# Loading the first attention head earlier in a one-core Trainium2 encoder kernel: second buffer, moved weight splits, reordered loads

## What is computed

```
kv = x @ w_kv;  k = rope(kv[:, :1024]);  v = kv[:, 1024:]      # 8 heads, two key maps of 64 per head
q  = rope(x @ w_q) * 64**-0.5
lam = exp(sum(lam0*lam1)) - exp(sum(lam2*lam3)) + lambda_init
p0, p1 = softmax(q0 @ k0.T), softmax(q1 @ k1.T)                # block-causal mask, per head
o  = rms_norm((p0 - lam*p1) @ v, g_norm) * (1 - lambda_init)
x  = layer_norm(ALPHA * x + o @ w_o)
```

## Time and profile before

| | us |
|---|---|
| runs | 2978.02 (median), 2977.02, 4519.82 |
| profiled execution, its time | 2981.81 |
| profiled execution, its span | 2980.0 |
| mean granted TensorE clock | 0.984 of full |
| TensorE busy | 2873.8 (96%) |

### The profile page before, as it was taken

How to read it: one execution, slowest core, us unless ns; L and a number is a source line. 1 busy time by engine, 2 the same in 40 slices (tenths; PEclk the granted TensorE clock), 3 DMA queues, 4 the chain that set the end, 5 groups by cost and what they waited for, 6 DMA issues and landing times. The chain is left out here.

```text
span 2980.0 us, 40342 instructions
## 1 busy us (share of the span) xinstructions
PE 2873.8 (96%) x15644; PEld 2543.4 (85%) x15644; DVE 1214.8 (41%) x2185; ACT 864.4 (29%) x1738; POOL 841.2 (28%) x939
## 2 busy tenths in 40 slices
PE   8999898999999999999999899988999999999997
PEld 8878777899988998897888688866899899989996
DVE  2256744632222222236513477743462222222226
ACT  2153241322211221122101278743241122112222
POOL 2112260521211121124212177831341111111114
PEclk9999998999999999999999999998999999999999
DMA  4111405111111111110232534294121111111101
GB/s 130 58 29 52 139 31 202 43 57 43 42 42 42 42 43 44 40 43 29 82 109 92 179 110 116 86 351 182 43 71 43 43 42 42 42 42 42 42 29 64
DMA packets 207186, 223.92 MB, mean 75 GB/s; under 512 B 42816, under 2 KB 151616, under 8 KB 207056
## 3 DMA queue, kind: packets, MB, share of 16 engines
q1 hardware_dynamic: 207056, 222.16, 23.0%
HBM read 184.90 MB, written 37.22 MB: 75 GB/s over the span
## 5 line engine op out<-in xcount | busy, mean ns | idle before, releaser
L792 POOL TENSOR_TENSOR wsplit<-raw,wsplit 128x1024 fp32r<-128x1024 f32 x192 | 459.4, 2395 | 1717.8 <-ACT wsplit L1030 1652.1
L1432 PE MATMUL ps<-xt,wsplit 128*128 128x384 f32 x5184 | 904.6, 334 | 1.4 <-DVE xt L1899 1.4
L1432 PEld LDWEIGHTS ps<-xt,wsplit 128*128 128x128 f32 x5184 | 899.1, 188 | 3.1 <-DVE xt L1899 1.8
L1623 PE MATMUL ps<-wsplit,hT 128*128 128x512 f32 x3456 | 787.7, 389 | 0.0
L1623 PEld LDWEIGHTS ps<-wsplit,hT 128*128 128x128 f32 x3456 | 649.0, 188 | 134.3
L1450 PE MATMUL ps<-wsplit,xt 128*128 128x512 f32 x2592 | 602.7, 393 | 2.8 <-DVE xt L1899 2.8
L1450 PEld LDWEIGHTS ps<-wsplit,xt 128*128 128x128 f32 x2592 | 487.9, 189 | 110.9 <-issue 6.5
L1030 ACT ACTIVATE wsplit<-raw 128x1024 fp32r<-128x1024 f32 x184 | 193.9, 1054 | 882.7 <-PE ps L1623 615.7
L2103 DVE TENSOR_TENSOR x_res<-x_res,ps 128x512 f32<-128x512 f32 x252 | 173.0, 687 | 434.8 <-PE ps L1623 434.8
L2155 DVE TENSOR_SCALAR hsq<-ps 128x384 f32<-128x384 f32 x192 | 107.0, 557 | 537.0 <-PE ps L1432 537.0
L1172 ACT ACTIVATE hsq<-hsq 128x384 f32<-128x384 f32 x192 | 101.1, 527 | 547.8 <-DVE hsq L2155 547.8
(11 more groups left out here) (186 smaller groups left out, 2365.1 us busy)
## 6 DMA issues: line engine op xcount, KB each, us to landing
raw<-in_w_up SPq DMA_DIRECT2D x64, 512.0 KB, 4.0
raw<-in_w_down SPq DMA_DIRECT2D x64, 512.0 KB, 3.7
Kc<-in_cache_k SPq DMA_DIRECT2D x8, 2048.0 KB, 10.1
Vc<-in_cache_v SPq DMA_DIRECT2D x8, 2048.0 KB, 10.1
raw<-in_w_in_a SPq DMA_DIRECT2D x24, 512.0 KB, 3.7
out<-kvs SPq DMA_DIRECT2D x36, 256.0 KB, 2.0
raw<-in_w_kv SPq DMA_DIRECT2D x16, 512.0 KB, 4.9
q_scr<-qst SPq DMA_DIRECT2D x16, 512.0 KB, 2.6
```

The source lines that it names most:

```text
L792: nc.gpsimd.tensor_tensor(wsplit[:, slot, 1, :], raw[:, slot, :], wsplit[:, slot, 0, :].bitcast(F32), ALU.subtract).then_inc(lo_done, 1)
L1432: last = nc.tensor.matmul(ps[0:M, b, 0:GW], st, xt[:, c, k, ng * GW:(ng + 1) * GW], start=(k == 0 and i == 0), stop=(k == KT - 1 and i == 2))
L1623: last = nc.tensor.matmul(ps[:, (v + t) % 6, :], hT[:, a, 2 * kp + k, tok:tok + P], wsplit[:, q, b, k * 512:(k + 1) * 512], start=(kp == 0 ...
```

## The change

The buffer `kqd2` is added, behind the query buffer in the region of the values; pairs 2 and 3 (the second half of head 0's tokens) use it, all others `kqd`. Pairs 0 and 2 (keys of head 0) and the two small loads for lambda and the norm gain are issued at the end of unit 3's turn in SP's program, pairs 1 and 3 (queries of head 0) after the stores of unit 4. Pair 4 now waits for the turns of pair 0 only, pair 5 for those of pair 1. SP no longer waits for the store of the last stream queries before the attention; those waits move to steps 16 and 40, with the load of `kqS`. The load of the first half of `w_o_b` moves behind the first values; its splits move to steps 6, 14, 22, 30 (ScalarE) and 8, 16, 24, 32 (GpSimd). Lambda's sums move to the start of unit 4 on DVE, its exponential ahead of unit 5's queries on ScalarE. At the end, attended tiles 0 to 5 are loaded ahead of `sample_out(6)`, tiles 6 and 7 after the last stream product, and then the last two outputs are stored.

```diff
@@ buffers
+    kqd2 = at("kqd2", O_V + 26624, [P, 2, 4, 2, 2, HD])
@@ SP: pair_in
-            if i >= 2:
-                sp.wait_ge(turned_full, 2 * i - 2)
+            kq = kqd2 if i in (2, 3) else kqd
+            if i >= 4:
+                sp.wait_ge(turned_full, 2 * i - 2 if i >= 6 else 2 * i - 6)
@@ SP: units of the products
-        load_p(G_O2, w_o_b[0], 0)
-        sp.wait_ge(ln_done, 2 * TILES)
-        for i in range(6):
-            sp.wait_ge(kv_out[i], 16 * 2 * TILES // 6)
-        pair_in(0)
+            if u == 3:
+                sp.wait_ge(ln_done, 2 * TILES)
+                for i in range(6):
+                    sp.wait_ge(kv_out[i], 16 * 2 * TILES // 6)
+                pair_in(0)
+                pair_in(2)
+                sp.dma_start(lamt[:], ...).then_inc(lam_in, 16)
+                sp.dma_start(gcol, ...).then_inc(lam_in, 16)
         for i in range(3):
             sp.wait_ge(q_out[i], 16 * ((PT - i + 2) // 3))
         pair_in(1)
-        sp.dma_start(lamt[:], ...).then_inc(lam_in, 16)
-        sp.dma_start(gcol, ...).then_inc(lam_in, 16)
+        pair_in(3)
         for t in range(TILES):
             kv_store(5, t)
         for i in range(6):
-            sp.wait_ge(kv_out[i], 16 * (6 if i % 3 < 2 else 7))
+            sp.wait_ge(kv_out[i], 16 * 6)
...
-        pair_in(2)
-        for i in range(3):
-            sp.wait_ge(q_out[i], 16 * Q_STORES[i])
-        pair_in(3)
         sp.wait_ge(g_full, GU_O2)
         values_in(0)
         pair_in(4)
+        pair_in(5)
         values_in(1)
-        pair_in(5)
         values_in(2)
+        load_p(G_O2, w_o_b[0], 0)
@@ SP: end of the stream attention
-        for b in range(STREAMS - 3, STREAMS - 1):
-            sample_out(b)
+        sample_out(STREAMS - 3)
         for i in range(2):
             sp.wait_ge(o_out[i], 16 * H_B * PT // 2)
         sp.wait_ge(smp_s_full, 2 * STREAMS)
-        for t in range(PT):
-            if t == 6:
-                sp.wait_ge(smp_pv, 2 * STREAMS)
-            sp.dma_start(oin[:, t, :], o_scr[t]).then_inc(tile_in[t], 16)
-        sample_out(STREAMS - 1)
+        for t in range(6):
+            attended_in(t)
+        sp.wait_ge(smp_pv, 2 * STREAMS)
+        for t in range(6, PT):
+            attended_in(t)
+        for b in range(STREAMS - 2, STREAMS):
+            sample_out(b)
@@ GpSimd, in step s
-            if 2 <= s < 6:
-                split_lo(G_O2 + s - 2)
+            if s % PT == 0 and 1 <= s // PT <= 4:
+                split_lo(G_O2 + s // PT - 1)
@@ ScalarE, in step s
-            if 0 <= s < 4:
-                split_hi_scaled(G_O2 + s)
+            if s % PT == 6 and s < 4 * PT:
+                split_hi_scaled(G_O2 + s // PT)
```

More of the change, by code:

```diff
@@ L647, in pair_in @@
                     for c in range(2):
-                        sp.dma_start(kqd[:, 0, :, c, dup, :], src[:, :, c]).then_inc(pair_loaded[0], 16)
+                        sp.dma_start(kq[:, 0, :, c, dup, :], src[:, :, c]).then_inc(pair_loaded[0], 16)
             else:
                 src = q_scr[4 * part:4 * part + 4, :, 2 * h:2 * h + 2].rearrange("t p c s d -> p t (c s d)")
-                sp.dma_start(kqd[:, 1].rearrange("p t c s d -> p t (c s d)"), src).then_inc(pair_loaded[1], 16)
+                sp.dma_start(kq[:, 1].rearrange("p t c s d -> p t (c s d)"), src).then_inc(pair_loaded[1], 16)
         def kv_store(u, t):
@@ L669, in _ @@
                     kv_store(u - 1, t)
-        load_p(G_O2, w_o_b[0], 0)
-        sp.wait_ge(ln_done, 2 * TILES)
-        for i in range(6):
-            sp.wait_ge(kv_out[i], 16 * 2 * TILES // 6)
-        pair_in(0)
+            if u == 3:
[4 more added lines that the diff above has]
+                pair_in(2)
+                sp.dma_start(lamt[:], lam[0:1].broadcast_to([P, 4, HD])).then_inc(lam_in, 16)
+                sp.dma_start(gcol, g_norm_b.rearrange("o v -> v o")).then_inc(lam_in, 16)
         for i in range(3):
@@ L678, in _ @@
         pair_in(1)
-        sp.dma_start(lamt[:], lam[0:1].broadcast_to([P, 4, HD])).then_inc(lam_in, 16)
-        sp.dma_start(gcol, g_norm_b.rearrange("o v -> v o")).then_inc(lam_in, 16)
+        pair_in(3)
         for t in range(TILES):
@@ L721, in _ @@
                 values_in(s // PT + 3)
-            if s == PT:
+            if s == 2 * PT:
+                for i in range(3):
+                    sp.wait_ge(q_out[i], 16 * Q_STORES[i])
+            if s == 5 * PT:
+                for i in (2, 5):
+                    sp.wait_ge(kv_out[i], 16 * 7)
                 sp.wait_ge(lo_done, G_O2 + 4)
@@ L752, in _, with attended_in @@
                 sample_out(b - 3)
-        for b in range(STREAMS - 3, STREAMS - 1):
-            sample_out(b)
+        def attended_in(t):
+            sp.dma_start(oin[:, t, :], o_scr[t]).then_inc(tile_in[t], 16)
+        sample_out(STREAMS - 3)
         for i in range(2):
@@ L1260, in _ @@
         split_hi(G_KVQ + 23)
+        act.wait_ge(lam_p, 2)
+        nc.scalar.activation(lam2, lam2, ACT.Exp).then_inc(lam_e, 1)
         for t in range(PT):
             query_hi(5, t)
-        act.wait_ge(lam_p, 2)
-        nc.scalar.activation(lam2, lam2, ACT.Exp).then_inc(lam_e, 1)
         def split_hi_scaled(g):
@@ L1735, in prepare @@
                 pe.wait_ge(*turned(i - 1 if i > 8 else i - 4))
+            kq = kqd2 if 4 <= i < 8 else kqd
             for k in range(4):
                 last = nc.tensor.transpose(ps[:, p_bank(i), k * P:(k + 1) * P],
-                                           kqd[:, int(mat == "q"), k, c].rearrange("p a d -> p (a d)"), ident)
+                                           kq[:, int(mat == "q"), k, c].rearrange("p a d -> p (a d)"), ident)
             last.then_inc(turned_full, 1)
@@ L2286, in query_lo, with lambda_sums @@
                                            ALU.mult, ALU.subtract).then_inc(q_split, 1)
+        def lambda_sums():
+            dve.wait_ge(lam_in, 32)
+            for i in range(2):
+                nc.vector.tensor_tensor(lamp[:, i, :], lamt[:, 2 * i, :], lamt[:, 2 * i + 1, :], ALU.mult).then_inc(dve_steps, 1)
+            dve.wait_ge(dve_steps, 2)
+            for i in range(2):
+                nc.vector.reduce_sum(lam2[:, i:i + 1], lamp[:, i, :], AX.X).then_inc(lam_p, 1)
+            nc.vector.tensor_scalar(gcol, gcol, 1.0 - LAMBDA_INIT, None, ALU.mult).then_inc(dve_steps, 1)
         nr = [0]
         for u in range(6):
+            if u == 4:
+                lambda_sums()
             for t in range(TILES):
@@ L2327, in _ @@
                     query_lo(2 * PT - 1)
[L2330 to L2336, removed]
         dve.wait_ge(lam_e, 1)
```

## The result

The kernel after takes 2966.88 us (median of six runs, 2965.61 to 2969.32), the kernel before 2980.12 us in six. One of the six took 4519.82 us, far outside the others; the ratio is taken from the fast runs alone. It is 0.9962 with an interval of 0.9951 to 0.9973, or 11.3 us less (8 to 14.6); the medians themselves stand 13.2 us apart. That is within the 2% named, and little more than half of the forecast -20.9 us. The profiled executions stand further apart, 2981.81 and 2965.61 us, spans 2980.0 and 2963.8: -16.2 us.

What follows compares the result with a forecast made beforehand. TensorE, busy 96% of the span, bounds the kernel, so only its idle time and slow clock can be won. Terms -9.2 - 10.6 + 7.2 - 8.3 = -20.9 us from 2978.0 us give 2957 us; range 2947 to 2970 us.

Steps and rivals of the forecast that it cites:

- start of attention, at step 3: First head's start: earlier loads end the 7.97 us DMA wait and turn 8's wait; step 3 comes 9.2 us sooner.
- first head from step 3: Head 0 after step 3: without its splits it runs like a mid head, 10.6 us less.
- splits in their new places: Boundaries of heads 0 to 3: ScalarE's pair costs 1.0 us, GpSimd's remainder 0.8 us each; 7.2 us more in all.
- output product starts, and its first 18 matmuls: End of stream attention: earlier tile loads start the product 8.3 us sooner; full clock and faster first 18 products bound it at 10.6.
- Rival 2: Pair 4 late, turn 8 waits 5.3 us more, and the clock drops at the end: 2964 us; chance 0.12.
- Rival 1: Moved splits paid in full, all 4.59 us per head on the path: 2968 us; chance 0.13.
- Rival 3: Moved splits cost nothing and the clock stays full at the end: 2948 us; chance 0.1.
- Rival 5: Attention start gains nothing because something else holds turn 4 back: 2966 us; chance 0.02.
- Rival 4: Slower: splits cost 4.59 us plus 1.7 us for the port per pair, first head unchanged: 2986 us; chance 0.03.
- the four places: Tests at attention's start, first head (17 to 19 us from step 3), moved splits, and output product (under 8 us gap).
- the one on the moved splits: Test: heads 0 to 3 last 1 to 3 us longer than 4 to 6, with boundary waits for ScalarE's copies and combination.
- three signs of error: Turn 8 waits over 2 us, heads 1 to 3 last over 32 us, or they show combinations over 2 us.

Runs made afterwards that it cites:

- after_again: The kernel after, unchanged, run again beside the version joining two repairs: 2967.14 us, ratio 0.9962 to before.
- a_no_lo: The kernel after with GpSimd's four remainders of the first half of w_o_b replaced by a tiny fill: 2959.09 us, ratio 0.9932 to before.
- b_splits: The kernel before with only the scaled splits of w_o_b spread over four heads, first-head loads as before: 2982.45 us, ratio 1.001 to before.
- a_splits_back: The kernel after with the splits and the load of w_o_b back in their old places: 2964.8 us, ratio 0.9948 to before.
- a_raw_pairs: The kernel after with pairs 4 and 5 loaded early into free raw slots, 6 and 7 sooner, w_o_b later: 2962.64 us, ratio 0.9941 to before.
- a_pair4_first: The kernel after with pair 4's key and query loads ahead of the first values in SP's program: 2965.22 us in one run.
- b_tiles: The kernel before with only the attended tiles loaded ahead of the last two stream outputs: 2970.96 us, ratio 0.9964 to before.
- a_hi_steps23: The kernel after with remainders in step 4, ScalarE's scaling in step 2 and rounding in step 3 of heads 1 to 4: 2964.5 us, ratio 0.9949.

## Why the prediction was wrong, and where it was right

The signs and places were right but for one. In the spans, with the second trace of the same kernel beside the first:

| term | forecast | after | after_again |
|---|---|---|---|
| start of attention, at step 3 | -9.2 | -6.9 | -5.7 |
| first head from step 3 | -10.6 | -9.4 | -10.1 |
| splits in their new places | +7.2 | +11.1 | +9.3 |
| output product starts, and its first 18 matmuls | -8.3 | -7.9, -1.9 | -7.2, +0.9 |
| sum | -20.9 | -15.0 | -12.8 |

In after the other 1.2 us to -16.2 lie mostly in the stream attention, 1.0 us shorter.

**The step that failed is "the splits in their new places".** ScalarE's part held in size: 1.0 us was forecast and 0.9 to 1.1 found; 0.56 us of it stand in the trace as TensorE's wait for the copy of turned queries. GpSimd's part was wrong in its mechanism. The forecast followed the remainder to the next balance and the combination on the same step, found the combination 0.8 us late at TensorE, and stopped there. In after the boundary pays nothing for it (a_no_lo leaves it at 4.77 to 4.86 us). The delayed combination is there, and TensorE takes it without a wait (VectorE and TensorE in head 1):

```profile
1729.36 0.49 DVE L2377 SCALAR_TENSOR_TENSOR PR<-PR,stats 128x256 f32<-128x256 f32 x1 [1.02 <-POOL stats L936]
```

```profile
1729.90 0.44 PE L1774 MATMUL ps<-cst,PR 128*128 128x128 f32 x2
```

This combination ends 12.3 us after the head's first scores, as late as the forecast had it (1801.5 to 1801.6 less 1789.3). But TensorE comes for it at 12.3 us too and no longer at 11.4 (1800.74): ScalarE's delay had already pushed it. So the forecast added two delays that overlap. That is read from these rows; no run has the remainder there without ScalarE's pair.

What it missed is `out_norm`, the other thing that GpSimd does in every step, whose result nobody needs soon, except that SP, in order, stands waiting to store it, with the next keys behind. The front text had said that SP works strictly in order, and the forecast did not follow the queue behind that wait. By a_no_lo 6.6 us went this way (4.8 by after_again) and 4.5 us are left, nearly all ScalarE's; forecast were 3.2 and 4.0.

The two split terms belong together. Forecast was a net -3.4 us; the traces say -9.4 + 11.1 = +1.7 in after and -0.8 in after_again. The attention stages say the same: b_splits against before +1.4 us, after and after_again against a_splits_back +1.6 and +0.3. So the move gained nothing, and of all terms this pair missed by the most.

**"The start of attention" was mis-sized.** Turn 8 was put at 1693.0 and came at 1695.56. Two numbers in it were taken from a quieter place: the four key issues took 3.15 us and not 2.03, with values ahead of them (SP's row of after is below), and from the last issue to the use passed 3.4 us and not 2.7. The row is pair 2. Pair 4 itself stands in the trace of before, and there its issues already took 2.95 us:

```profile
1697.13 2.95 SPq L648 DMA_DIRECT2D kqd<-out  x4
```

The lower bound of 4 to 7 us in the text holds the measured 6.9, but not by its reason: `w_o_b` does not slow pair 4, for in a_splits_back, where it is loaded long before, turn 8 waits 3.02 us. Rival 2 had late loads as its mechanism and priced it at 5.3 us; counted from the first turn it was 2.3. In a_raw_pairs and a_pair4_first, with pair 4 sooner, turn 8 waits only 0.51 and 0.66 us. The first head's term fell 1.2 us short for a like reason, 1.07 us of it the wait in step 5 for pair 6.

**The output product was right in its mechanism**: the gap is gone, turning follows at once, and 7.7 us were measured from turning to product where 7.2 were reckoned. The clock's part came on top in the profiled execution, where the range had named 2 us for it. That was luck: in after_again the clock fell and this part was lost (see the last section).

**The rivals.** Rival 1 (4.59 us per split on the path) saw the danger and no mechanism; 2.8 were paid. Rival 3 had the splits hidden, which they were not. Rival 5 is out: the first scores came 7.6 us sooner. Rival 4 asked for combinations held up by GpSimd's port; in heads 1 to 4 no combination lasts longer than its size asks, 1024 columns 1.28 us and 768 columns 1.01 us in the groups by shape:

```profile
L2377 DVE SCALAR_TENSOR_TENSOR PR<-PR,stats 128x1024 f32<-128x1024 f32 x5 | 6.4, 1276 | 0.0
...
L2377 DVE SCALAR_TENSOR_TENSOR PR<-PR,stats 128x768 f32<-128x768 f32 x4 | 4.0, 1009 | 0.0
```

So the remainder's place behind `out_norm` did keep the two apart, as argued, and the 3153 ns of the earlier trace rows have no successor. By the 1009 ns here, 2.1 us were lost in that combination, and not the 1.7 of the forecast.

**Of its own tests**, three of the four places came out as written; the one on the moved splits did not (heads 1 to 4 are the longer ones and not 0 to 3, two of them by over 3 us, with a wait in step 5 that it does not name). Of its three signs of error one is there: turn 8 waits over 2 us. The range held the median; the point did not.

## What to carry to other kernels

Moving work to an engine with idle time is priced by following every result of that engine that is now later, down to those that nobody seems to need soon: a store in an in-order DMA queue carries that delay to each load behind it. Put loads ahead of stores that wait, and before spreading work over quiet stages, ask what the same amount costs there: here nine to ten microseconds in one head became nine to eleven over four. Two delays that one engine suffers at the same place are not added before it is asked whether one hides the other. A DMA issue is priced from the row of that very transfer, if the trace has one.

## What the runs showed of the hardware that was not expected

**Issuing the same four key DMAs took SP between 2.03 and 5.46 us.** They took 2.03 us in the earlier trace rows, 2.08 to 2.15 in most heads, and here in after 3.15 us behind values and 5.46 us behind four weight loads:

```profile
1688.97 3.15 SPq L650 DMA_DIRECT2D kqd<-out  x4
1694.73 4.97 SPq L539 DMA_DIRECT2D raw<-in_w_o_b  x4
1699.74 5.46 SPq L650 DMA_DIRECT2D kqd<-out  x4
```

The Trainium skill (Perfetto Trace Analysis, DMA Instruction — HWDGE) says that the profiled time of such an issue runs until all its descriptors are made and that an engine begins on them early when the buffer is full. That fits these rows; no run here separates a full buffer from other causes. The DMA share was 0.97 in the stretch of the 3.15 us and 1.05 in that of the 5.46, against 0.40 in the earlier trace rows and 0.61 and 0.67 in heads 1 and 5. The share is not all of it: pair 4 in before took 2.95 us at 0.47 and keys in b_splits 3.52 us at 0.40. Nor are the values: with pair 4 ahead of them (a_pair4_first) its issues still took 2.59 us, and in after_again, the same program as after, 4.73.

**The clock at the output product differs between executions of one kernel.** after and after_again are the same program. In after the granted clock was full (2.4 GHz) in the 4 us before the product and in it; in after_again it stood at the lower level, 1.2 GHz, in the 4 us before. A row of each window table:

```profile
2045.00:2050.00 5.00, 4.59 (x22) 3.76 (x23) 0.36 (x1) 0.00 (x0) 0.00 (x0) 1.00 0.26 77
```

```profile
2040.00:2044.00 4.00, 1.94 (x8) 1.57 (x8) 2.54 (x4) 1.69 (x3) 0.00 (x0) 0.50 0.91 346
```

The first 18 matmuls took 4.42 us in after and 7.17 us in after_again:

```profile
2044.18 7.17 PE L1457 MATMUL ps<-wsplit,xt 128*128 128x512 f32 x18 [1.41 <-DVE xt L1907]
```

TensorE's longest pause ahead of it is the same in both, 1.85 and 1.84 us. These 2.75 us come and go between executions, not much less than the runs of after differ (2965.61 to 2969.32), so the 1.9 us of the span's gain is not the change's alone. The other traces show the same two ways. Of the eleven with the new order at the end, six keep the full clock, start the product 7.63 to 7.65 us after the last stream product and take 4.38 to 4.42 us for the 18; in five (b_tiles, a_splits_back, a_raw_pairs, a_hi_steps23, after_again) the clock falls on the way, the start comes after 8.02 to 8.36 us and the 18 take 5.93 to 7.17 us. What decides it stays open.
